# Delta rule on one core: where v's correction, the squares and their sums, the root and the second heads' scale rows stand in the last halves

## What is computed

```python
def chunk_gated_delta_rule(q, k, v, g, beta):
    ...
    a = jnp.where(strict, jnp.einsum('bhnid,bhnjd->bhnij', k_beta, k) * decay, 0.0)
    sol = lax.linalg.triangular_solve(a + eye, rhs, left_side=True, lower=True, unit_diagonal=True)
    ...
    def step(state, xs):
        v_new = u_c - jnp.einsum('bhck,bhkv->bhcv', w_c, state)
        o = jnp.einsum('bhck,bhkv->bhcv', q_c, state) + jnp.einsum('bhij,bhjv->bhiv', attn_c, v_new)
        state = state * last_c[..., None, None] + jnp.einsum('bhck,bhcv->bhkv', k_c, v_new)
        return state, o

def gated_deltanet(h, w_in, w_conv, a_log, dt_bias, w_norm, w_out):
    ...
    o = chunk_gated_delta_rule(q, k, v, g, beta)
    o = rms_norm(o, w_norm) * jax.nn.silu(z.reshape(b, t, GDN_V_HEADS, GDN_HEAD_DIM).astype(jnp.float32))
    return o.reshape(b, t, GDN_V_DIM).astype(h.dtype) @ w_out
```

## Time and profile before

| | us |
|---|---|
| median of 3 runs | 2701.93 |
| the profiled execution | 2700.45 |
| its span in the trace | 2698.7 |
| PE busy | 2526.5 (94%) |
| DVE busy | 1400.2 (52%) |
| ACT busy | 846.7 (31%) |
| POOL busy | 254.7 (9%) |

### The profile page before, as it was taken

The page is one execution under the profiler, slowest core; times in us unless marked ns, Lnnn a source line. Parts: engine busy times, 40 slices in busy tenths (PEclk is TensorE's granted clock), DMA queues, the critical chain, the costliest instruction groups (busy, mean ns, idle before and its releaser), DMA issues.

```text
span 2698.7 us, 39276 instructions
## 1 busy us (share of the span) xinstructions
PE 2526.5 (94%) x16016; PEld 2218.1 (82%) x16016; DVE 1400.2 (52%) x1907; ACT 846.7 (31%) x1216; POOL 254.7 (9%) x198
## 2 busy tenths in 40 slices
PE   6999999998999999989988999998997788899998
PEld 6999999988999999989876788886884445688886
DVE  6777655555544344542555666666117364534433
ACT  4423444443322122412222322223223353323322
POOL 2000232222100000200101000002003101100001
PEclk9999999888999999999777999998997899899999
DMA  3223433324222222222001444552320000222221
GB/s 129 78 81 84 127 73 88 81 61 176 79 94 79 94 93 83 103 67 91 16 0 72 162 146 164 176 175 72 117 78 16 0 0 16 78 94 93 93 94 63
DMA packets 93861, 235.31 MB, mean 87 GB/s; under 512 B 60074, under 2 KB 61700, under 8 KB 69556
## 3 DMA queue, kind: packets, MB, share of 16 engines
q1 hardware_dynamic: 88208, 201.40, 22.8%
q10 hardware_dynamic: 5540, 32.30, 3.4%
HBM read 222.00 MB, written 11.67 MB: 87 GB/s over the span
## 4 chain that ended last, share of the span: by engine, by line
PE 84%; DVE 9%; ACT 3%; issue 2%; DMA 1%; DVEq 0%; ACTq 0%; POOL 0%; POOLq 0%; SPq 0%
PE ps L298 65%; PE ps L1083 1%; PE ps L462 1%; PE ps L1095 1%; PE ps L1071 1%; PE ps L302 1%; PE ps L2388 1%; PE ps L2370 1%; PE ps L1837 1%; PE ps L1838 1%; DVE a_mx L2454 1%; PE ps L1108 1%; PE ps L1107 1%; DVE n_y L443 1%; PE ps L486 1%
## 5 line engine op out<-in xcount | busy, mean ns | idle before, releaser
L298 PE MATMUL ps<-xa_hi,whi 128*128 128x264 f32 (+1 forms) x2512 | 654.8, 320 | 47.4 <-DVE wlo L321 20.4
L298 PE MATMUL ps<-xa_lo,whi 128*128 128x264 f32 (+1 forms) x2512 | 649.4, 318 | 0.0
L298 PE MATMUL ps<-xa_hi,wlo 128*128 128x264 f32 (+1 forms) x2512 | 647.0, 317 | 0.0
L321 DVE TENSOR_TENSOR wlo<-raw,whi 128x2048 fp32r<-128x2048 f32 x161 | 369.8, 2297 | 255.3 <-ACT whi L314 252.6
L298 PEld LDWEIGHTS ps<-xa_hi,whi 128*128 128x128 f32 x2512 | 416.8, 190 | 91.6 <-DVE wlo L321 22.6
L314 ACT ACTIVATE whi<-raw 128x2048 fp32r<-128x2048 f32 x161 | 307.5, 1910 | 575.8 <-PE ps L298 564.5
L298 PEld LDWEIGHTS ps<-xa_lo,whi 128*128 128x128 f32 x2512 | 416.9, 190 | 29.5
L298 PEld LDWEIGHTS ps<-xa_hi,wlo 128*128 128x128 f32 x2512 | 416.3, 190 | 29.9
L298 PE MATMUL ps<-xb_hi,whi 128*128 128x264 f32 (+1 forms) x1280 | 385.0, 341 | 7.4 <-DVE xb_lo L1954 5.6
L298 PE MATMUL ps<-xb_lo,whi 128*128 128x264 f32 (+1 forms) x1280 | 385.9, 342 | 0.0
L298 PE MATMUL ps<-xb_hi,wlo 128*128 128x264 f32 (+1 forms) x1280 | 384.3, 341 | 0.0
(11 more groups left out here) (407 smaller groups left out, 2883.1 us busy)
## 6 DMA issues: line engine op xcount, KB each, us to landing
raw<-weights SPq DMA_DIRECT2D x161, 1024.0 KB, 4.9
mod_w<-weights_mod ACTq DMA_DIRECT2D x24, 1024.0 KB, 4.8
g_EC<-scr_g SPq DMA_DIRECT2D x10, 424.0 KB, 5.0
scr_z<-z_st SPq DMA_DIRECT2D x16, 264.0 KB, 4.5
g_D<-scr_g SPq DMA_DIRECT2D x10, 371.0 KB, 5.2
scr_a<-g_AT SPq DMA_DIRECT2D x10, 318.0 KB
h<-x_in ACTq DMA_DIRECT2D x4, 528.0 KB, 8.3
z_b<-scr_z SPq DMA_DIRECT2D x1, 2112.0 KB
```

Source lines behind the costliest of these rows:

```text
L298: mm = pe.matmul(ps[:, at_ + step * c + bank, 0:tn], w[:, hb.slot, k, c * P:(c + 1) * P], x[:, k, t0:t0 + tn], start=(k == 0 and n == 0), ...
L321: dve.tensor_tensor(wlo[:, hb.slot], raw[:, hb.raw_slot], whi[:, hb.slot].bitcast(F32), ALU.subtract).then_inc(S("w_lo"), 1)
```

## The change

- In halves 6 to 9 DVE corrects v before it decays the queries. In half 9 the decay stands behind the second merge's update of `g_U`.
- ACT squares half t - 1 behind the evictions of v of half t, in every half.
- In halves 6 to 9 PE takes half t - 1's sums between kS and P. `SUMS_IN` keeps five entries, for halves 0 to 4.
- In half 9 the root, the transposes to rows and their copies stand behind the first merge's evictions and XU. ACT takes one root of a single element ahead of that merge, which puts the load of the root's table there.
- The second heads: the row's transposes go into tile 1 of j = 0, its copy behind four of the eight gates, the load of weights ahead of it on SP no longer waits, and `some` takes tiles 8 and 9 behind j = 0, 10 to 12 behind j = 1, 13 to 15 behind j = 2.

```diff
         CHUNK_END = HALVES - 2
-        SUMS_IN = {(6, 0): 0, (6, 1): 2, (6, 2): 4, (7, 0): 6, (7, 1): 1, (7, 2): 3, (8, 0): 5, (8, 1): 7}
+        LATE_SUMS = N_Z - Z_EARLY
+        SUMS_IN = {(6, 0): 0, (6, 1): 1, (7, 0): 2, (7, 1): 3, (8, 0): 4}
@@ pe_gdn
                 z = t + Z_EARLY
+                if t >= LATE_SUMS:
+                    for x in range(2):
+                        if t < HALVES - 1:
+                            pe.wait_ge(S("g_A"), nth(t + 1, x))
+                        mm = sums(t - 1, x)
                 if t == HALVES - 1:
-                    sums(t - 1, 0)
-                    sums(t - 1, 1).then_inc(S("head_sums"), 4)
+                    mm.then_inc(S("head_sums"), 4)
@@
-                    if l == 0 and t == HALVES - 1:
-                        roots_rows()
                     for x, g in groups_of(t):
                         pe.wait_ge(S("g_Pc"), 2 * MERGES * t + 2 * l + x + 1)
@@
                         mm.then_inc(S("g_XU"), 1)
+                    if l == 0 and t == HALVES - 1:
+                        roots_rows()
@@
-                          between=last_sums if first else last_roots_rows if (g, j) == (0, 1) else None)
+                          between=last_sums if first else None, during=((1, 5), last_roots_rows) if first else None)
@@ act_gdn
                     act.activation(heads4(g_VT, x, w=P), four_of(4 * x + 3, w=P), ACT.Copy).then_inc(S("g_vt"), 1)
+                if t:
+                    for x in range(2):
+                        squares(t - 1, x)
                 if t >= CHUNK_END:
                     silu(range(0, 4) if t == CHUNK_END else range(4, 8))
                 if t == HALVES - 1:
-                    act.wait_ge(S("head_inv"), 3)
-                    act.activation(head_stat[0:CH, 0:72], head_stat[0:CH, 0:72], ACT.Sqrt).then_inc(S("head_rstd"), 1)
+                    act.activation(misc[0:1, 7:8], ones[0:1, 0:1], ACT.Sqrt)
@@
                     if l == 0 and t == HALVES - 1:
+                        act.wait_ge(S("head_inv"), 3)
+                        act.activation(head_stat[0:CH, 0:72], head_stat[0:CH, 0:72], ACT.Sqrt).then_inc(S("head_rstd"), 1)
                         act.wait_ge(S("head_sums"), 16 + 8)
@@ dve_gdn
             def half(t):
                 more = t < HALVES - 1
                 z = t + Z_EARLY
+                if t < LATE_SUMS:
+                    decayed_queries(t)
                 for x, g in groups_of(t):
                     residual(t, x, g)
+                if LATE_SUMS <= t < HALVES - 1:
+                    decayed_queries(t)
@@
                         ins.then_inc(S("g_Uup"), 1)
+                    if l == 1 and not more:
+                        decayed_queries(t)
@@ sp_gdn
-            next_load(ONE_RAW_END + 1)
+            load(ONE_RAW_END + 1)
             sp.wait_ge(S("z_in"), 16 * 9)
             sp.wait_ge(S("head_st"), 16 + 16)
@@ act_gdn_out
             for t in range(N_Z, 2 * N_Z):
+                if t == N_Z + 4:
+                    act.wait_ge(S("head_sums"), 32)
+                    act.activation(on_row[0:8, 4 * CH:T], ps[0:8, 6, 0:T - 4 * CH], ACT.Copy).then_inc(S("head_st"), 8)
                 act.activation(z_tile(t), z_tile(t), ACT.Silu).then_inc(S("two_act"), 1)
             act_split(act, HalfBlock(HB_GDN_OUT + N_Z + 2))
-            act.wait_ge(S("head_sums"), 32)
-            act.activation(on_row[0:8, 4 * CH:T], ps[0:8, 6, 0:T - 4 * CH], ACT.Copy).then_inc(S("head_st"), 8)
+            act_gated_high(act, range(KT, KT + 2))
             act_split(act, HalfBlock(HB_GDN_OUT + N_Z + 3))
-            act_gated_high(act, range(KT, KT + 4))
+            act_gated_high(act, range(KT + 2, KT + 5))
             act_split(act, HalfBlock(HB_GDN_OUT + N_Z + 4))
-            act_gated_high(act, range(KT + 4, 2 * KT))
+            act_gated_high(act, range(KT + 5, 2 * KT))
@@ dve_gdn_out
-            for j in range(4):
+            for j, ready in enumerate((range(KT, KT + 2), range(KT + 2, KT + 5), range(KT + 5, 2 * KT), ())):
                 dve_down(dve, "two_ev", HalfBlock(HB_GDN_OUT + N_Z + j), j, FULL)
-                if j == 1:
-                    some(range(KT, KT + 4))
-                if j == 2:
-                    some(range(KT + 4, 2 * KT))
+                if ready:
+                    some(ready)
```

23 lines of the change are left out of this document (14 added, 9 removed).

## The result

| | before | after |
|---|---|---|
| median of 4 runs, us | 2701.74 (2700.31 to 2705.76) | 2679.95 (2676.63 to 2683.86) |
| the profiled execution | 2700.45 | 2683.86 |
| its span in the trace | 2698.7 | 2681.9 |
| PE busy | 2526.5 | 2522.7 |

The ratio is 0.9918, 95% interval 0.99 to 0.9935: faster by 21.8 us. The forecast was 12.3 us, 2689.5, in a range from 2681.5 to 2696. The sign and the place were right; the time lies 1.5 us under the range. So the prediction was wrong in its size, and most of what follows asks why. The same changed kernel, timed twice more, gave 0.9949 and 0.992, so one question is how much of the 21.8 us belongs to the change.

A forecast was written before the change was run, and what follows sets the result against it. PE bounds the kernel with 84% of the chain of waits, its largest hole in half 9. Terms 9.3 + 4.3 + 0.4 - 1.7 = 12.3 us gave 2689.5 us on the median's scale, range 2681.5 to 2696.

The forecast's parts named there:

- Half 9, 9.3 us: Half 9: correcting v before the decay removes most of PE's 8.75 us wait ahead of the rows of roots; gain 9.3 us.
- The charge of one slow window (1.7): New half 9: one low-clock window of 3.4 us charged at 1.7 us; bounds none and three (5.1).
- rival 1: Half 9: DVE's reciprocal is held by POOL's gates, costing 4.2 us; gain 8.1, time 2693.8; chance 8%.
- Halves 6 to 8, 4.3 us: Moved sums and DVE's new order gain 3.3 us in half 6, 1.0 in half 7, 0 in half 8; bounds 1 and 9.
- the 0.45 that I charged for the lost cover: Halves 6 and 7: a 0.45 us wait each for DVE's last update, no longer covered by sums behind the third merge.
- the bounds of -1 to +0.7: Half 8: net gain taken as 0, between -1 and +0.7 us, as ACT's squares make P's eviction 1.0 later.
- Second heads, 0.4 us: Output projection: earlier rows replace a 2.85 us wait at j = 3 by 2.5 at j = 2; gain 0.4 us.
- my own bounds (+4.5): Second heads: gain 4.5 us if the rows land before 659.6, from the 2.85 us wait and a slow window of 1.7.
- rival 3: Clock gives back: four low-clock windows (6.8 us) behind third merges and j = 3 go; time 2682.7; chance 14%.
- the rows' early landing (2685): Second heads' rows of roots land before 659.6, gaining 4.5 us; 2685 was the low end of the forecast's own spread.
- Rivals 2, 4 and 5: Slower clock in halves 6 to 9, 2694.6, 12%; decay still meets POOL, 2698.8, 3%; late second-head rows, 2709, 3%.
- Behind 692 us: Later stages are unchanged and on PE, so they only move; a change of more than 3 us there would disprove the prediction.

The follow-up runs named there:

- the experiment with POOL's start: Kernel before, with POOL's eight gates of half 9 made to wait until the queries are decayed: 2693.6 us, 0.9971.

## Why the prediction was right, and where it failed

**Half 9, 9.3 us: right, mechanism and size.** Rows 3 to 6 were read rightly: the decay was held by POOL (the experiment with POOL's start), the correction and the reciprocal are not, and nothing else was as long as the hole. Where the clock is full, half 9 gained 35.1 - 23.8 = 11.3 against the trace that I had worked from, 2.0 more than the 9.3. Of these 1.8 lie behind the second merge's transpose, where my steps ended (15.7 us from there to the output projection before, 13.9 after). The trace before has a second low stretch there, which I left out and which costs 1.7:

```profile
627.00:630.40 3.40, 3.40 (x18) 3.32 (x17) 1.02 (x2) 0.00 (x0) 0.00 (x0) 0.50 0.02 6
```

Four of the five traces of the changed kernel have none in half 9. The waits of 0.9 and 1.0 came as 0.79 and 0.83. The charge of one slow window (1.7) came in no trace: four had none, and the fifth 10.2 us at 0.50, which made it 3.7 us longer. That is 0.7 in the mean, and the mean gain was 9.9 and not 7.6. In the first trace of after, half 9 gained 35.1 - 27.5 = 7.6, exactly the forecast, because that trace is the one with the long low stretch: luck.

**The reciprocal, rival 1: refuted.** 0.60 us beside POOL. The rule quoted from the Trainium skill, "SBUF — State Buffer", section "Who interferes with whom", that a single SBUF input does not contend, agrees with the row. Its other sentence, that the loser waits for one instruction, agrees with half 0 (2.48 to 2.51 us beside one instruction of 2.4 to 2.5) and with the turns taken in the kernel with the decay first again. It does not cover the decay of half 9 before: 7.13 to 7.34 us, six gates, in four traces. So a hold by a train of instructions of the other engine is to be priced at either end.

**Halves 6 to 8, 4.3 us: right in the sum (4.4), wrong in the parts.** Half 6 gained 5.8 instead of 3.3. Its wait and its slow sums went as worked out, and the 0.45 that I charged for the lost cover did not come. With them went low clock, which I had left to the bounds: 0.76 in the window before and 0.89 after, that is 35.6 x 0.24 = 8.5 us less 30.1 x 0.11 = 3.3 us of lost length; part of the 3.3 forecast is in that. Undoing the sums or undoing the order each costs 4 of the 5.8, with a clock of 0.80 in half 6 either time, so the two overlap. Why the clock rises only with both is not shown. Half 8 lost 1.9, outside the bounds of -1 to +0.7. The wait for the update is 1.38 to 1.52 us in the five traces in place of 0.45. I had read 0.45 off half 8's row before and taken it for the new cover too, and did not follow DVE's line, where the last inverses stand ahead of the update. The wait ahead of the first merge's XU fell from 0.90 to 0.30 and gives 0.6 of that back. The rest is low clock: two traces of five have 32.9 us at a mean clock of 0.79, the other three 28.7 to 29.5 at 0.88.

**Second heads, 0.4 us: the step that failed.** It gained 4.3 in each of the five traces, at the end of my own bounds (+4.5), which I named and did not take. (The other bound, -2.6, was added up wrongly: its own terms give -3.9.) The term came from two rows of transfers at another load: write 3.69 and broadcast 9.71, for which I took 2.5 and 9.71. The chain of waits after:

```profile
633.54 1.23 DMA scr_r<-on_row
634.78 8.46 DMA qkv<-scr_r
```

The copy of the row came when I had said. The write took 1.23 us where I had 2.5, the broadcast 8.46 where I had 9.71, and the rows landed 2.5 us sooner than I had reckoned, which is all of j = 2's wait. On PE it is down to

```profile
647.06 0.48 PE L298 MATMUL ps<-xa_hi,whi 128*128 128x264 f32 x2 [0.24 <-DVE h L652]
```

With the wait the low stretch behind it went as well, in all five traces. The old write had been issued 1.3 us behind a load of 1024 KB, and the DMA engines were busy for 62% of its time; the new one comes 14.7 us behind that load, at 7%. Seven traces with the old place have 3.50 to 3.91 us for the write and 9.70 to 9.85 for the broadcast, six with the new one 1.23 to 1.25 and 8.31 to 8.46. Taking the old place back, with all that belongs to it, brought 3.50 and 9.74 back and the loss of 4.1 us with them; that it was the load alone no run separates. I had moved the write to a place and kept most of the price of the old place.

**The sum.** 17.6 us up to j = 7 instead of 12.3: 3.9 of the 5.3 from the second heads, the rest from half 6 and half 9 less half 8 and the later start. Less 3.9 behind it this is 13.7 by the traces. Three timings gave 21.8, 12.8 and 21.2, mean 18.6, and the profiled executions are not the timed ones. So the change gives between 13 and 22 us, the forecast of 12.3 is short of its middle by some 5, and about 3 us of the 21.8 are above the mean of the same kernel. A gain of 18.6 would have been 2683.3, inside the range: that the first timing fell out of it, by 1.5 us, is in part the scatter of the timing, while the term of the second heads is wrong in every trace. **The range** failed because I let the clock gain (rival 3, 2682.7) and the rows' early landing (2685) stand as alternatives. Both came, at least in part. Together, with the low stretch behind j = 3 counted once, they give 2689.5 - 6.8 - 2.4 = 2680.3. A low end needed both gains in one case, and room for a timing as far from its mean as the first one.

**Rivals 2, 4 and 5** did not come. The clock was not worse in any trace as a sum over halves 6 to 9, the decay never met POOL, and the rows landed at 643.2, with DVE waiting 3.24 us for them and PE 0.24. **Behind 692 us**, I had said that a change of over 3 us would prove me wrong: it changed by 3.9 in the mean of five traces against four, and the cause is open.

## What to carry to other kernels

When two engines read SBUF side by side, look in the timeline for an instruction of many times its usual length beside a train on the other engine: taking the hold away alone gave 7.2 us here, and moving the held instructions behind what PE waits for 12 to 14, more than everything that was done around it. When a step is moved, price its transfers by rows with the same company, not by its own old rows, and if the old rows stand behind a big load, take a third of the write at one end of the range (1.23 against 3.69 here). Where a stage's gap and its low clock stand side by side, put the gain of both into one case, and take several traces before a stretch of low clock is charged or credited.
